# One instruction form, three orders of work and a choice of PSUM banks in a transformer kernel

## What is computed

```python
for layer in (0, 1):                       # first_block
    h = h + (hybrid_mixer if layer == 0 else conformer_conv)(rms_norm(h))
    h = h + (silu(hn @ wg) * (hn @ wu)) @ wd      # hn = rms_norm(h), wg, wu: 1024x2816, wd: 2816x1024
h = h + 0.5 * swiglu_ffn(rmsnorm(h))       # second_block
h = h + (gate0 * (ret @ w_ret_up) + gate1 * (pool @ w_pool_up)) @ w_out   # retention and pooling
h = h + 0.5 * swiglu_ffn(rmsnorm(h))
return rmsnorm(h)
```

## Time and profile before

| | |
|---|---|
| median of 3 runs | 1228.37 us (1228.21 to 1228.70) |
| the profiled execution's own time | 1228.21 us |
| its span | 1226.2 us |
| TensorE (PE) busy | 1201.3 us, 98% |
| VectorE (DVE) busy | 913.0 us, 74% |
| ScalarE (ACT) busy | 672.9 us, 55% |
| GpSimd (POOL) busy | 164.2 us, 13% |
| moved by DMA | 220.71 MB, 180 GB/s |

### The profile page before, as it was taken

How to read it: one execution, slowest core, us unless ns; L and a number is a source line. 1 busy time by engine, 2 the same in 40 slices (tenths; PEclk the granted TensorE clock), 3 DMA queues, 4 the chain that set the end, 5 groups by cost and what they waited for, 6 DMA issues and landing times.

```text
span 1226.2 us, 14255 instructions
## 1 busy us (share of the span) xinstructions
PE 1201.3 (98%) x5534; PEld 983.5 (80%) x5534; DVE 913.0 (74%) x1124; ACT 672.9 (55%) x810; POOL 164.2 (13%) x171
## 2 busy tenths in 40 slices
PE   7999999999998999999999999999999999999997
PEld 6776878888887878888878888888888888788885
DVE  6656788888669788887688887655477656888873
ACT  6564656655645556664556654655434444666541
POOL 2400012220010012220012220000000000222200
PEclk9999999999999999999999999999999999999999
DMA  9422465555541555555555555654553354555540
GB/s 338 168 99 90 150 248 193 188 187 197 214 172 35 202 206 184 188 185 189 186 206 195 186 187 187 266 192 177 185 201 137 139 204 142 208 187 189 192 164 35
DMA packets 32327, 220.71 MB, mean 180 GB/s; under 512 B 3730, under 2 KB 4130, under 8 KB 6531
## 3 DMA queue, kind: packets, MB, share of 16 engines
q1 hardware_dynamic: 32258, 219.79, 49.3%
HBM read 218.72 MB, written 1.05 MB: 179 GB/s over the span
## 4 chain that ended last, share of the span: by engine, by line
PE 90%; DVE 4%; issue 2%; ACT 2%; POOL 2%; DMA 0%; SPq 0%; POOLq 0%; DVEq 0%; ACTq 0%
PE ps L258 28%; PE ps L260 28%; PE ps L259 28%; PE ps L263 3%; PE ps L266 3%; POOL st L379 1%; DVE wlo L217 1%; DVE FS L677 1%; DMA raw<-in_w 0%; POOL AR L868 0%; ACT whi L210 0%; ACT xh L346 0%; DVE raw L668 0%; DVE AR L670 0%; DVE AR L666 0%
## 5 line engine op out<-in xcount | busy, mean ns | idle before, releaser
L217 DVE SCALAR_TENSOR_TENSOR wlo<-raw,whi 128x2048 fp32r<-128x2048 f32 x166 | 380.5, 2293 | 126.2 <-ACT whi L210 94.6
L258 PE MATMUL ps<-whi,xh 128*128 128x512 f32 x1120 | 443.1, 396 | 3.6 <-DVE wlo L232 3.2
L260 PE MATMUL ps<-whi,xl 128*128 128x512 f32 x1120 | 437.3, 390 | 0.0
L259 PE MATMUL ps<-wlo,xh 128*128 128x512 f32 x1120 | 437.2, 390 | 0.0
L210 ACT CAST whi<-raw 128x2048 fp32r<-128x2048 f32 x163 | 312.2, 1916 | 178.9 <-PE ps L260 176.9
L258 PEld LDWEIGHTS ps<-whi,xh 128*128 128x128 f32 x1120 | 210.7, 188 | 53.5 <-DVE xl L363 3.3
L260 PEld LDWEIGHTS ps<-whi,xl 128*128 128x128 f32 x1120 | 210.7, 188 | 45.1
L259 PEld LDWEIGHTS ps<-wlo,xh 128*128 128x128 f32 x1120 | 211.0, 188 | 41.2
L258 PE MATMUL ps<-whi,yh 128*128 128x512 f32 x352 | 142.7, 406 | 4.5 <-DVE yl L653 3.3
L260 PE MATMUL ps<-whi,yl 128*128 128x512 f32 x352 | 138.2, 393 | 0.0
L259 PE MATMUL ps<-wlo,yh 128*128 128x512 f32 x352 | 137.9, 392 | 0.0
(11 more groups left out here) (215 smaller groups left out, 1179.7 us busy)
## 6 DMA issues: line engine op xcount, KB each, us to landing
raw<-in_w SPq DMA_DIRECT2D x199, 1024.0 KB, 4.8
raw<-in_w SPq DMA_DIRECT2D x4, 256.0 KB, 5.9
raw<-in_w SPq DMA_DIRECT2D x2, 512.0 KB, 7.5
AR<-in_b_pw SPq DMA_DIRECT2D x1, 1024.0 KB, 4.7
AR<-in_gate_bias SPq DMA_DIRECT2D x1, 1024.0 KB, 8.2
out<-AR SPq DMA_DIRECT2D x2, 512.0 KB, 2.6
AR<-in_dft SPq DMA_DIRECT2D x1, 864.0 KB, 8.9
AR<-in_rmask SPq DMA_DIRECT2D x1, 768.0 KB, 9.8
```

Source lines behind the costliest of these rows:

```text
L217: e.scalar_tensor_tensor(out=wlo[:, v % S, :], in0=raw[:, v % R, :], scalar=1.0, in1=whi[:, v % S, :].bitcast(F32), op0=ALU.mult, op1=ALU. ...
L258: e.matmul(o, ah, bh, start=start, stop=False, skip_group_check=skip)
L259: e.matmul(o, ah, bl, start=False, stop=False, skip_group_check=skip)
L260: return e.matmul(o, al, bh, start=False, stop=stop, skip_group_check=skip)
```

## The change

It has five parts:

1. `lo` and `lo_quarter` write `wlo` by `tensor_tensor` (raw - whi) instead of `scalar_tensor_tensor` (raw * 1.0 - whi).
2. In the feed-forward stages ScalarE does `hi` of unit u0+5 ahead of `scalar_turned`, and from step 2 on `scalar_sums` first of all in a step.
3. VectorE writes `wlo` of unit u0+5 in quarters around `vector_turned` and the gate, does `vector_sums` directly after `vector_turned`, and puts the second quarter of unit d+2 ahead of the gate.
4. In the hybrid stage TensorE's transposes of `sq` come one and two quarters earlier, `tensor_gate_rank` comes ahead of a quarter, and ScalarE's order follows.
5. The retention output adds up in the banks that all other stages use, instead of the same banks in the other order.

```diff
@@ lo, and lo_quarter in the same way
-                e.scalar_tensor_tensor(out=wlo[:, v % S, :], in0=raw[:, v % R, :], scalar=1.0,
-                                       in1=whi[:, v % S, :].bitcast(F32), op0=ALU.mult,
-                                       op1=ALU.subtract).then_inc(*sig.up("lo", v))
+                e.tensor_tensor(wlo[:, v % S, :], raw[:, v % R, :], whi[:, v % S, :].bitcast(F32),
+                                ALU.subtract).then_inc(*sig.up("lo", v))
@@ scalar_ffn
             hi_half(e, q, u0 + 4, 1)
+            hi(e, q, u0 + 5)
             scalar_turned(e, q, f, 0)
             for j in range(1, FAST + 1):
                 d = ff_down(u0, j - 1)
-                if j > 1:
+                if j == 1:
+                    scalar_gate_ffn(e, q, f, 1, 0)
+                    scalar_mixed(e, q, f, 0)
+                    scalar_sums(e, q, f, 0)
+                else:
+                    scalar_sums(e, q, f, j - 1)
                     hi(e, q, d + 1)
-                scalar_mixed(e, q, f, j - 1)
-                scalar_gate_ffn(e, q, f, j, 0)
-                if j == 1:
-                    hi(e, q, d + 1)
-                scalar_sums(e, q, f, j - 1)
+                    scalar_mixed(e, q, f, j - 1)
+                    scalar_gate_ffn(e, q, f, j, 0)
                 hi(e, q, d + 2)
                 scalar_gate_ffn(e, q, f, j, 1)
@@ vector_ffn
             for k in range(4):
                 lo_quarter(e, q, u0 + 4, k, "hi_half" if k < 2 else "hi")
+            lo_quarter(e, q, u0 + 5, 0)
+            lo_quarter(e, q, u0 + 5, 1)
             vector_turned(e, q, f, 0)
             vector_gate_ffn(e, q, f, 1, 0)
+            lo_quarter(e, q, u0 + 5, 2)
+            lo_quarter(e, q, u0 + 5, 3)
             vector_mixed(e, q, f, 0)
-            lo(e, q, u0 + 5)
             vector_mix(e, q, f, 1)
             vector_sums(e, q, f, 0)
             vector_gate_ffn(e, q, f, 1, 1)
@@ vector_ffn, steps 2 to 8
                 lo(e, q, d)
                 vector_turned(e, q, f, j - 1)
+                vector_sums(e, q, f, j - 1)
                 lo(e, q, d + 1)
                 vector_gate_ffn(e, q, f, j, 0)
-                vector_sums(e, q, f, j - 1)
                 vector_mixed(e, q, f, j - 1)
                 if j < FAST:
                     vector_mix(e, q, f, j)
                 lo_quarter(e, q, d + 2, 0)
+                lo_quarter(e, q, d + 2, 1)
                 vector_gate_ffn(e, q, f, j, 1)
-                lo_quarter(e, q, d + 2, 1)
                 lo_quarter(e, q, d + 2, 2)
                 lo_quarter(e, q, d + 2, 3)
@@ tensor_hybrid
             quarter(e, q, "sk", u, 0, 1, 4, xh, xl, x)
+            tensor_heads(e, q, "sq", 0)
             quarter(e, q, "sk", u, 1, 0, 5, xh, xl, x)
-            tensor_heads(e, q, "sq", 0)
+            tensor_heads(e, q, "sq", 1)
             quarter(e, q, "sk", u, 1, 1, 5, xh, xl, x)
             u = U["sv"]
             quarter(e, q, "sv", u, 0, 0, 4, xh, xl, x)
-            tensor_heads(e, q, "sq", 1)
             quarter(e, q, "sv", u, 0, 1, 4, xh, xl, x)
             tensor_heads(e, q, "sk", 0)
+            tensor_gate_rank(e, q)
             quarter(e, q, "sv", u, 1, 0, 5, xh, xl, x)
             tensor_heads(e, q, "sk", 1)
-            tensor_gate_rank(e, q)
             tensor_z_scores(e, q, 0)
@@ scalar_hybrid
             scalar_heads(e, q, "sk", 0)
+            scalar_heads_turned(e, q, "sq", 0)
             hi(e, q, 6)
-            scalar_heads_turned(e, q, "sq", 0)
+            scalar_heads_turned(e, q, "sq", 1)
             scalar_heads(e, q, "sk", 1)
             hi(e, q, 7)
-            scalar_heads_turned(e, q, "sq", 1)
             scalar_plain(e, q, "sv", 0)
             scalar_heads_turned(e, q, "sk", 0)
+            scalar_gate_rank(e, q)
             scalar_heads_turned(e, q, "sk", 1)
-            scalar_gate_rank(e, q)
             scalar_z_scores(e, q, 0)
@@ retention; everywhere ACC = ((0, 1), (2, 3))
-        RACC = ((2, 3), (0, 1))
-                    out_part(e, q, "ret", u + n, t, 2 * n, xh, xl, RACC[t], first=n == 0)
+                    out_part(e, q, "ret", u + n, t, 2 * n, xh, xl, ACC[t], first=n == 0)
-            residual(e, q, "ret", "n1", 0, RACC[0])
+            residual(e, q, "ret", "n1", 0, ACC[0])
```

More of the change, by code:

```diff
@@ L241, in lo_quarter @@
             cols = slice(UC // 4 * k, UC // 4 * k + UC // 4)
-            e.scalar_tensor_tensor(out=wlo[:, v % S, cols], in0=raw[:, v % R, cols], scalar=1.0,
-                                   in1=whi[:, v % S, cols].bitcast(F32), op0=ALU.mult,
-                                   op1=ALU.subtract).then_inc(*sig.up("lo", v) if k == 3 else sig.up("lo_quarter", v, k))
+            e.tensor_tensor(wlo[:, v % S, cols], raw[:, v % R, cols], whi[:, v % S, cols].bitcast(F32),
+                            ALU.subtract).then_inc(*sig.up("lo", v) if k == 3 else sig.up("lo_quarter", v, k))
         def hi_half(e, q, v, k):
@@ L2154, in tensor_ret @@
             q.wait_ge(*banks.emptied("x", "merge", 0, 1))
-            out_part(e, q, "ret", u + 2, 0, 4, xh, xl, RACC[0])
-            out_part(e, q, "ret", u + 3, 0, 6, xh, xl, RACC[0], last=True)
+            out_part(e, q, "ret", u + 2, 0, 4, xh, xl, ACC[0])
+            out_part(e, q, "ret", u + 3, 0, 6, xh, xl, ACC[0], last=True)
             q.wait_ge(*banks.emptied("x", "merge", 1, 1))
-            out_part(e, q, "ret", u + 2, 1, 4, xh, xl, RACC[1])
+            out_part(e, q, "ret", u + 2, 1, 4, xh, xl, ACC[1])
             turn_x(e, q, "n2", "ret", 0, 0)
             turn_x(e, q, "n2", "ret", 0, 1)
-            out_part(e, q, "ret", u + 3, 1, 6, xh, xl, RACC[1], last=True)
+            out_part(e, q, "ret", u + 3, 1, 6, xh, xl, ACC[1], last=True)
         def scalar_ret(e, q):
@@ L2317, in vector_ret @@
             lo(e, q, RU["out"] + 5)
-            residual(e, q, "ret", "n1", 0, RACC[0])
+            residual(e, q, "ret", "n1", 0, ACC[0])
             norm_dve(e, q, "n2", 0)
-            residual(e, q, "ret", "n1", 1, RACC[1])
+            residual(e, q, "ret", "n1", 1, ACC[1])
             lo(e, q, RU["out"] + 6)
```

## The result

The changed kernel takes 1239.09 us (median of 4 runs, 1237.92 to 1241.63), the kernel before 1228.29 beside it (1227.29 to 1228.70): ratio 1.0092, 95% interval 1.0073 to 1.0111. The forecast was 1236.5 and its range 1232 to 1244. The profiled execution took 1238.23 us, with a span of 1236.4.

The account below looks back on a forecast made before the run. TensorE, busy for 1201.3 of 1226.2 us, was taken as the bound. Banks 1.5, hybrid stage 3.3 and feed-forward stages 4 x (1.36 - 0.5) summed to 8.2 us on 1228.21: forecast 1236.5, 80% range 1232 to 1244.

Parts of the forecast that it names:

- The banks, +1.5: Retention stage: TensorE waits 2.07 us for line 1910 to empty bank 1, the 0.56 wait for line 411 vanishes: +1.5.
- The hybrid stage, +3.3: Hybrid stage: three new delays of 2.08, 1.57 and 1.0 us, less old waits of 0.22 and 1.18: +3.3.
- (a): Hybrid stage: transposes of `sq` 0 move ahead of a quarter, so TensorE waits for GpSimd's product: 2.08 us.
- (b): Hybrid stage: transposes of `sq` 1 follow one quarter later and wait for GpSimd's product: 1.57 us.
- (c): Hybrid stage: with `tensor_gate_rank` moved ahead, the first scores wait for the `sk` 1 transposes' evacuation: +1.0 us.
- The price of a wait, its idle time plus 0.16: Any TensorE wait: delays the stream by its idle time plus 0.16 us, from a matmul bar of 0.39.
- Step 1, -0.5 each: Feed-forward stages, j = 1: later `vector_turned` costs TensorE 0.5 us, the 0.99 wait for `sums_lo` goes: -0.5 per stage.
- Step 2, +1.36 each: Feed-forward stages, j = 2: GpSimd's held fourth addition delays sums cast, next cast, remainder and gate: +1.36 us per stage.
- Steps 3 to 8, 0 by a tie of 0.07: Feed-forward stages, j = 3 to 8: GpSimd's fourth addition takes the port 0.07 us before VectorE's `lo`: 0 us.
- VectorE winning every tie: Rival, chance 0.12: in feed-forward steps 3 to 8 VectorE gets the port first, 32.6 us more, 1269.
- The free port: Rival, chance 0.05: the new instruction doesn't hold GpSimd back; -0.9 to +0.9 us, 1228.2 at the middle.
- the stalls given back: Rival, chance 0.08: later TensorE waits absorb the hybrid stage's 3.3 us, leaving 4.9, so 1233.

Follow-up runs that it names:

- Parts 1 and 4: The kernel before with only the new instruction form: 1228.41 us, ratio 1.0002; with only the new hybrid-stage order: 1231.43 us, ratio 1.0031.
- part 5 alone: The kernel before with only the retention output's banks changed: 1231.25 us, ratio 1.0026.
- the experiment with the third quarter: The changed kernel with the second quarter of unit d+2 put back behind the gate, so three quarters lie behind it: 1274.61 us, ratio 1.0373.
- the run with the other moves: The kernel before with `vector_sums` directly behind `vector_mixed`, `tensor_gate_rank` in two halves, and line 411's remainder ahead of `vector_merge`: 1225.44 us, ratio 0.9977.

## Why the prediction was right, and where it was off

- *The sign and the mechanism*: right. Parts 1 and 4 and the stall of part 5 alone cost in the trace what the sum says, and none of the losses is given back later. The feed-forward stages cost 6.3 where the sum has 3.4: the waits were the forecast ones, two of the terms were too small.
- *The other instruction, 0*: right (+0.3, within its interval of 1).
- *The banks, +1.5*: 1.5 in the profiled execution. What the sum didn't have is the clock: part 5 alone costs 3.1 in the median, and its removal from the changed kernel saves 2.2.
- *The hybrid stage, +3.3*: 3.0. (a) 2.08 was 2.25, (b) 1.57 was 1.57, (c) 1.0 was 0.8, and the old waits of 0.22 and 1.18 gave back 0.4 and 1.2.
- *The price of a wait, its idle time plus 0.16*: too small by 0.1, as said above. The old waits were worth 4 x 1.1, 1.2 and 0.7, some 6.3 and not 5.7. The error stands on both sides of the sum and cancels in part.
- *Step 1, -0.5 each*: this is the term that was most mis-sized. It came out at -0.1 in the changed kernel (+1.00, then -1.09 to -1.12), and the loss lies above the upper bound of 0.8. `vector_turned` ended at 162.50 (165.52 less the 3.02 of the hybrid stage), at the bound of 162.5 and not near the 162.2 that 0.5 stands for: the estimate let GpSimd's additions hold `vector_turned` alone, while they held the two quarters ahead of it too (1.56 for 1.26). TensorE followed 0.15 behind it where 0.05 was reckoned, and the restart cost 0.1. That is 1.6 us of the 2.6 between forecast and median.
- *Step 2, +1.36 each*: 1.69, by the chain forecast. TensorE comes to that quarter 0.1 earlier by what step 1 won, the chain ends 0.1 later (184.85 less 3.02 is 181.83, for 181.74), and the restart costs 0.1. That is 1.3 us more. The hybrid stage takes 0.3 back.
- *Steps 3 to 8, 0 by a tie of 0.07*: right, and the tie is real. The same 0.07 stands in the trace, and turned to -0.11 it costs 34 to 36 us. The rule of the Trainium skill (page "SBUF — State Buffer", section "Who interferes with whom"), that whoever issues first keeps the pair to its end, agrees with both sides of it.
- *The rest*: 1.5 for the banks, 3.0 and 6.3 make 10.8, which is also what the medians differ by. TensorE's end in the trace is only 10.2 later. Between ffn0 and ffn1 0.6 comes back that the change has no part in: there every kernel here, the one before too, has a stretch at half clock behind idle time of TensorE, and it is not equally long. Windows of the kernel before, and then of the changed one:

```profile
396.00:398.00 2.00, 2.00 (x6) 1.52 (x6) 2.00 (x5) 1.97 (x6) 0.00 (x0) 0.50 0.00 0
398.00:400.00 2.00, 2.00 (x8) 1.55 (x6) 1.34 (x4) 0.45 (x2) 0.00 (x0) 0.63 0.31 70
```

```profile
400.00:402.00 2.00, 2.00 (x5) 1.54 (x6) 2.00 (x4) 1.97 (x6) 0.00 (x0) 0.50 0.00 0
402.00:405.00 3.00, 3.00 (x17) 2.51 (x16) 1.70 (x5) 0.73 (x3) 0.00 (x0) 0.84 0.45 104
```

Over the fourteen profiled executions this place alone moves TensorE's end by up to 0.8 us either way against the kernel before. And the four timed runs of the changed kernel are two near 1237.9 with a mean clock of 0.997 and two at 1240.2 and 1241.6 with 0.994, with the median in the gap between them. So that 10.8 comes out to the tenth is in part luck; that the slower pair had the retention stage's slow stretch would fit, and I haven't shown it run by run.

- *The rivals*: VectorE winning every tie is what the experiment with the third quarter is, 1274.6 where 1269 was priced from the unchanged base of 1236.5. The free port and the stalls given back are out. (Against the latter the prediction said that TensorE's largest waits are for VectorE and GpSimd; its largest single one is 3.8 us for a DMA of constants at the start.)

Open: why the clock falls behind the retention stall in some executions and not in others, the profiled one of the changed kernel among them, which has the same stall.

## What to carry to other kernels

A wait of the bounding engine is not a fault in itself: asking earlier for something whose producer hasn't moved only turns work that covered a wait into a stall. Before moving an engine's work, write down who holds the port shared by VectorE and GpSimd at that moment and by how much; where urgent work stands behind a GpSimd instruction, a lead of 0.07 us can be worth 1.4 us a time, and where VectorE would have the port, a wait that gives it to GpSimd first can win most of the loss back (1.1 of 1.7 us here). And when a wait is removed, look for the next place where the same engine has to be in time: the slack there decides how much of the gain stays.

## What the hardware showed that was not expected

- A 128x2048 subtraction is 2.293 us in either form, `scalar_tensor_tensor` or `tensor_tensor`, over 166 instances each, and both hold GpSimd's 128x128 addition (0.46 alone) up to 2.50.
- A GpSimd addition that is held ends 0.3 us after the VectorE instruction's end; a VectorE pass held by a GpSimd addition of 0.46 takes 0.25 longer. GpSimd gets in between two VectorE passes in a row, one addition at each seam, and is held again by the next pass (2.51 and 2.51 in the run with the other moves).
- A single idle stretch of TensorE of some 2 us was followed, in the profiled execution of two of the five kernels that have it, by a stretch at half clock (1.2 GHz) that cost 1.6 us more. With part 5 alone that doubled the price of the banks' stall.
- A wait of TensorE delayed its stream by the idle time and 0.2 to 0.3 us more, since the first matmul behind it has a bar of 0.47 to 0.50 where the others have 0.39.
